# Rows of the first three expert passes fetched by token number, in a two-layer encoder with routed experts

## The reference

```python
def hier_moe(h, w_group, w_router, w_gate, w_up, w_down):
    """Top-1 expert group, then top-2 experts inside it; gated-MLP experts."""
    g_probs = softmax(t @ w_group); g_sel = argmax(g_probs)
    e_logits = (t @ w_router) of the chosen group     # 4 groups of 4 experts
    top_p, top_i = lax.top_k(softmax(e_logits), 2)
    weights = g_w * top_p / sum(top_p)
    a = jnp.einsum('td,edf->tef', t, w_gate)
    u = jnp.einsum('td,edf->tef', t, w_up)
    hid = jax.nn.silu(a) * u * gates[:, :, None]
    y = jnp.einsum('tef,efd->td', hid, w_down)
```

## Time and profile before

| | us |
|---|---|
| median of 3 runs | 1138.62 (1138.2 to 1141.27) |
| the profiled execution, its own time | 1140.07 |
| its span, first to last instruction | 1138.4 |
| mean granted TensorE clock | 0.972 of full speed |
| PE busy | 1050.2 |

### The profile page before, as it was taken

One profiled execution on the slowest core, in us unless ns is written; L12 is line 12 of the kernel. 1 busy time (PEld: TensorE's weight loads), 2 busy tenths in 40 slices (PEclk: granted clock), 3 DMA queues, 4 the chain that ended last, 5 costly groups with the idle time before them and its releaser, 6 DMA issues.

```text
span 1138.4 us, 16440 instructions
## 1 busy us (share of the span) xinstructions
PE 1050.2 (92%) x6553; PEld 662.3 (58%) x6553; DVE 446.1 (39%) x806; ACT 263.5 (23%) x528; POOL 240.5 (21%) x232
## 2 busy tenths in 40 slices
PE   4999999999999999978999998989998978999982
PEld 4989979989988877753333332454444443333321
DVE  6400314224226540155132226557547745232216
ACT  5132143134224411020011111314214510111111
POOL 5333314205214533003000005510000002000004
PEclk9999999999999999988999998989999998999997
DMA  7232223114115121367899887030004058998945
GB/s 305 74 130 75 75 90 114 56 42 161 56 37 168 37 74 74 148 278 285 313 358 376 353 361 259 42 148 0 1 1 148 1 233 339 333 380 323 403 189 222
DMA packets 34838, 201.01 MB, mean 177 GB/s; under 512 B 4352, under 2 KB 4352, under 8 KB 25808
## 3 DMA queue, kind: packets, MB, share of 16 engines
q1 hardware_dynamic: 21168, 151.26, 34.7%
q10 hardware_dynamic: 8864, 31.74, 7.9%
q0 software_dynamic: 4736, 17.04, 4.1%
HBM read 303.70 MB, written 28.44 MB: 292 GB/s over the span
## 4 chain that ended last, share of the span: by engine, by line
PE 79%; DVE 12%; issue 3%; DMA 2%; ACT 2%; POOL 1%; SPq 0%; POOLq 0%; DVEq 0%; ACTq 0%
PE ps L844 30%; PE ps L1083 15%; PE ps L1102 7%; PE ps L969 4%; PE ps L1207 4%; PE ps L1149 3%; PE ps L850 3%; DVE arena L2079 2%; PE ps L1071 2%; DVE arena L2076 2%; PE ps L1060 1%; PE ps L912 1%; ACT arena L1522 1%; PE ps L1167 1%; DMA ring<-in_w_ret 1%
## 5 line engine op out<-in xcount | busy, mean ns | idle before, releaser
L844 PE MATMUL ps<-x_hi,ring_r 128*128 128x264 f32 x1024 | 190.9, 287 | 3.2 <-DVE xT L1562 3.1
L2159 POOL TENSOR_TENSOR ring_r<-ring,ring_r 128x1024 fp32r<-128x1024 f32 x56 | 136.9, 2459 | 260.5 <-ACT ring_r L1299 260.4
L844 PEld LDWEIGHTS ps<-x_hi,ring_r 128*128 128x128 f32 x1024 | 160.3, 190 | 3.6 <-issue 3.3
L1083 PE MATMUL ps<-arena,xT 128*32 128x512 f32 x864 | 158.0, 600 | 0.0
L1083 PE MATMUL ps<-ring,xT 128*32 128x512 f32 x672 | 143.9, 602 | 5.9 <-DVE xT L1562 5.9
L844 PE MATMUL ps<-xT_r,ring_r 128*128 128x264 f32 x512 | 146.2, 286 | 0.0
L1562 DVE TENSOR_TENSOR xT<-ps,gains 128x512 f32<-128x512 f32 (+1 forms) x76 | 46.9, 660 | 182.8 <-PE ps L1071 177.3
L844 PE MATMUL ps<-ring_r,x_hi 128*128 128x512 f32 x320 | 100.6, 395 | 0.0
L844 PEld LDWEIGHTS ps<-xT_r,ring_r 128*128 128x128 f32 x512 | 97.0, 189 | 0.1
L1102 PE MATMUL ps<-arena 128*32 128x512 f32 x624 | 87.3, 595 | 4.3 <-ACT arena L1436 4.3
L1299 ACT ACTIVATE ring_r<-ring 128x1024 fp32r<-128x1024 f32 x56 | 57.9, 1054 | 118.4 <-PE ps L844 70.8
(11 more groups left out here) (265 smaller groups left out, 1554.7 us busy)
## 6 DMA issues: line engine op xcount, KB each, us to landing
arena<-in_w_gu SPq DMA_DIRECT2D x22, 2048.0 KB, 14.8
ring<-in_w_gu SPq DMA_DIRECT2D x20, 2048.0 KB
arena<-in_w_down SPq DMA_DIRECT2D x36, 1024.0 KB
arena<-in_w_gu POOLq DMA_DIRECT2D x18, 2048.0 KB
ring<-in_w_gu POOLq DMA_DIRECT2D x14, 2048.0 KB
arena<-in_w_down POOLq DMA_DIRECT2D x26, 1024.0 KB
ring<-in_w_ret SPq DMA_DIRECT2D x48, 512.0 KB, 3.7
ring<-in_w_ret_out SPq DMA_DIRECT2D x16, 512.0 KB, 4.9
```

Source lines behind the costliest of these rows:

```text
L844: last = mm(dst, a_parts[x], b_parts[y], start=(start and n == 0), stop=(stop and n == 2))
L1083: last = mm(ps[cols, b, :], xgT[:, k % 2, c, cols], by_row(gu(j))[:, c, :], start=(c == 0), stop=(c == KT - 1))
L2159: G.tensor_tensor(w_lo[slot][:, m], w_raw[slot][:, m], w_hi[to][:, m], ALU.subtract).then_inc(lo_made, 1)
```

## The change

- **Rows by token number.** ScalarE stores the normalized rows to device memory (token_rows), tile by tile, as soon as they are made. For each of passes 0, 1 and 2 VectorE makes a one-hot table of slots and tokens (slots_of_pass), PE multiplies it with a column of token numbers (tokens_of), ScalarE turns the result into integers, and POOL fetches the 128 rows with one indirect load (gather_rows). The product of the one-hot table with the rows, and ScalarE's copy of it, are gone. Passes 3 to 11 read slot_rows as before.
- **VectorE's order.** The places in the pairs are worked out first, from the pair counts alone, then pass 0's table, then the rows of e_of for the pairs, then the rest, with slot_i, pass 1's table, the rows of e_of for the singles, pass 2's table. Pass 0's rows are scaled by ScalarE.
- **POOL's order.** First gather, six scatters, second gather, the other scatters, the reading and loading for pass 0's singles, third gather.
- **Slots.** ROWS_SLOT becomes 5, so that pairs 3 and 4 of pass 2 are guessed and only pair 5 of pass 3 waits for the scatters. The first half of W_q (attention) is loaded behind the last gathers.
- **ScalarE.** The row load of pass 3 (load_rows(3)) stands ahead of the copy of pass 0's hidden values and waits for the scatters.
- **Products of constants.** Five ahead of the mask, five ahead of the token numbers, five behind them, instead of nine behind the ranks.

```diff
-ROWS_SLOT = 3
-GUESSED = [4, 5, 0, 1, 2]
+ROWS_SLOT = 5
+GUESSED = [0, 1, 2, 3, 4]
+GATHERED = 3
...
+                constant_products(5)
                 n = EXPERTS * (5 - l)
                 pe.wait_ge(m["mask_ready"], 1)
...
-                for _ in range(9):
-                    mm(ps[:, 4, :], ident, con[:, 0:512], start=True, stop=True)
-
-
-                pe.wait_ge(m["slot_ready"], 2)
-                for c in range(2):
+
+                def tokens_of(k):
+                    pe.wait_ge(hot_ready, GATHERED * l + k + 1)
                     for i, t in enumerate(tiles):
-                        last = mm(ps[:, c, :], one_hot[0:rows(t), t, :], xn[0:rows(t), t, 512 * c:512 * c + 512],
+                        last = mm(ps[:, B_TOKENS[k], 0:1], one_hot[k][0:rows(t), t, :], con[0:rows(t), C_TOKEN + t:C_TOKEN + t + 1],
                                   start=(i == 0), stop=(i == len(tiles) - 1))
-                last.then_inc(full[0], 1)
+                    last.then_inc(tokens_made, 1)
+
+                constant_products(5)
+                tokens_of(0)
+                constant_products(5)
...
+                        if k == 0 and c == KT // 2:
+                            tokens_of(1)
...
                 rows_to_features(0)
                 gate_up(0)
                 rows_to_features(1)
+                tokens_of(2)
...
+                def store_rows(n):
+                    t = MOE_TILES[l][n]
+                    act.wait_ge(nrm[f"_m{l}"]["xn_done"], n + 1)
+                    act.dma_start(token_rows[128 * t:128 * t + rows(t), :], xn[0:rows(t), t, :]).then_inc(rows_stored, 16)
...
-                fl.wait_full(act, f"X0_{l}")
-                nc.scalar.activation(xg[:, 0, :], flat(ps[:, 0:2, :]), ACT.Copy).then_inc(free[0], 1)
-                act.wait_ge(m["scattered"], 16 * 2 * (5 - l))
-                load_rows(1)
+                def tokens_of(k):
+                    act.wait_ge(tokens_made, GATHERED * l + k + 1)
+                    nc.scalar.activation(token_i[:, l, k:k + 1], ps[:, B_TOKENS[k], 0:1], ACT.Copy).then_inc(tokens_read, 1)
...
+                tokens_of(0)
+                first_features()
+                tokens_of(1)
                 tanh_of(0)
-                load_rows(2)
+                tokens_of(2)
                 for k in range(1, ROUNDS):
+                    if k == 1:
+                        act.wait_ge(m["scattered"], 16 * 2 * (5 - l))
                     load_rows(k + 2)
...
+                def gather_rows(k):
+                    pool.wait_ge(tokens_read, GATHERED * l + k + 1)
+                    if k == 0:
+                        pool.wait_ge(rows_stored, 16 * (5 * l + len(tiles)))
+                    if k == 2:
+                        round_full(pool, l, B_ROWS, 0)
+                    G.indirect_dma_start(xg[:, k % 2, :], None, token_rows,
+                                         bass.IndirectOffsetOnAxis(token_i[:, l, k:k + 1], 0)).then_inc(rows_gathered[k], 16)
```

More of the change, by code:

```diff
@@ L737, in first_weights @@
                     gate_up_weights(l, j, j)
-                rest = [j for j in (0, 1, 2, 4, 5) if j not in ready]
+                rest = [j for j in GUESSED if j not in ready]
                 for j in rest[:2]:
@@ new lines, in experts, with slots_of_pass @@
+                step.wait()
+                for n in range(2):
+                    step.done(V_.tensor_reduce(first_place[:, n, 0:nt], in_pairs[:, n], X, ALU.add))
+                step.wait()
+                iota = con[:, C_IOTA:C_IOTA + 128]
+                def slots_of_pass(k, where, numbers):
+                    for t in range(nt):
+                        step.done(V_.tensor_scalar(one_hot[k][:, t, :], numbers, where[:, 0, t:t + 1], None, ALU.is_equal))
+                    step.wait()
+                    for t in range(nt):
+                        last = V_.scalar_tensor_tensor(one_hot[k][:, t, :], numbers, where[:, 1, t:t + 1], one_hot[k][:, t, :],
+                                                       ALU.is_equal, ALU.add)
+                    last.then_inc(hot_ready, 1)
```

189 lines of the change are left out of this document (117 added, 72 removed).

## The result

The changed kernel takes 1143.8 us (median of 19 runs, 1140.66 to 1146.85), the kernel before 1138.53 (19 runs, 1137.04 to 1142.52): ratio 1.0039, 95% interval 1.003 to 1.0049. It is 0.4% **slower**; predicted was 1132.6. The profiled execution took 1144.62 (before 1140.07), its span is 1142.8 (before 1138.4).

A forecast was written before the change was run, and what follows sets the result against it. PE was taken as the bound, with a serial stretch ahead of the expert passes deciding pass 2's gate/up; 2.5 us earlier in layer 0 plus 3.5 in layer 1 made 6.0, so 1138.62 becomes 1132.6, range 1127.5 to 1138.5.

The forecast's parts named there:

- Products of constants, gain 1.1: Ahead of the mask: five constant products hold PE's clock up, so VectorE starts on the counts 1.1 us earlier.
- First table at 518.3: Layer 0's routing: VectorE has pass 0's one-hot table ready at 518.3 us, before it was 525.66.
- First gather, lands 5.2 after its issue: Pass 0's rows, layer 0: issued at 520.1, landing 525.3, bounds 3.1 to 7.3 us; pass 0's gate/up at 528.8.
- rival B: First gather waits for row stores behind guessed weights, starts at 524.5, pass 0 at 533; 1138 us, chance 0.15.
- slot_i at 528.1: Layer 0: the slot numbers are ready at 528.1 us, 4.9 later than before, as first-pass work goes ahead.
- Second gather at 536.0: POOL's queue, layer 0: seventh transfer, issued at 536.0, its numbers in time at 535.6, landing by 540.
- POOL's value loads are bare, 4.0 us: Ahead of pass 1: four value loads (3.2) and two issues (0.8) follow POOL's eleventh transfer; gate/up 1 at 546.0.
- rival C: POOL's loads cost next to nothing and the second gather's rows decide: pass 1 at 543, 1127 us, chance 0.05.
- Low clock at pass 1: 1.5 in layer 0, none in layer 1: Gate/up 1 starts at 1.2 GHz in layer 0, giving back 1.5 us; layer 1's shorter wait costs no clock.
- Third gather, hidden in both layers with 3.1 to 7.3 us: Pass 2's rows: in layer 0 issued at 546.2, landed by 553.5 beside slot-5 weights, needed at 554.9, so no wait.
- Rival D: Third gather beside slot-5 weights lands after 16.4 us; pass 2 comes 5 late, layer 1 5.8; 1149 us, chance 0.08.
- Passes 3 to 11 as before: Behind pass 2 nothing waits and all moves by the same amount; a wait there would make the forecast wrong altogether.

The follow-up runs named there:

- no_early_products: The changed kernel without the five products of constants ahead of the mask: 1145.39 us, ratio 1.0047 to the kernel before.
- hold_in_best: The fastest follow-up kernel (1132.08 us) with the slot-5 weights issued only when pass 3's rows have landed: 1135.18 us, ratio 0.9961 to the kernel before.
- rows3_late: The changed kernel with pass 3's row load issued behind ScalarE's copy of pass 0's hidden values: 1143.47 us, ratio 1.0041 to the kernel before.

## Why the prediction was wrong, point by point

- *Products of constants, gain 1.1.* Right in kind, 2.4 GHz at the rank products (1.21 instead of 2.21); size 2.0 in the trace of no_early_products, and its median can't confirm it.
- *First table at 518.3.* Right: 518.5.
- *First gather, lands 5.2 after its issue.* In layer 0 it took 6.5 (520.48 to 527.0), inside the bounds: 1.3 late. **In layer 1 it took 8.7**, outside them (the upper one was 7.3), for I had given layer 1 no landing of its own; pass 0's gate/up came 2.7 late there. It is not rival B, whose sign was POOL idle until the rows' stores land: POOL issued as soon as it had the numbers. ScalarE's copies took 2.18 (2.2 predicted). Pass 0's gate/up started 1.7 late and took 1.1 more than I had (it ended at 541.5): some five and a half of its sixteen half steps ran at 1.2 GHz, not three and a half as before; PE had stood 2.7 and 2.4 us ahead of it.
- *slot_i at 528.1.* Right to 0.1.
- *Second gather at 536.0.* 538.40: the numbers came 2.8 us late, from the two delays above, and four scatters stood behind them. I had named POOL's queue as the bound but not that a wait in its middle delays the scatters' end, and so the slot-5 weights.
- *POOL's value loads are bare, 4.0 us.* **Wrong.** The loads are issued between two scatters. The bound 0 was missing; I had taken SP's rows for another engine's. This is the mechanism of rival C, at 0.05, and so is its sign, gate/up 1 released by VectorE. By the Trainium skill (DMA: Bandwidth & Descriptors, "Latency and other measured facts") four of them would have cost 2.4 us; no run here shows what one takes, only that four add nothing here, where the issues behind them stand between the scatters. Pass 1 came at 545.7 against 546.0 because this error and the late second gather cancel in layer 0, which is luck. In layer 1 they don't, as the first gather took 3.5 longer than I had it: pass 1 gained 1.0 (1.3 with the 0.3 of layer 0), not 3.5.
- *Low clock at pass 1: 1.5 in layer 0, none in layer 1.* It came in both, 1.6 and 1.7. The gap of 2.5 us that I had read as leaving the clock up before holds 1.1 us of transposes; PE stood 1.47 in it.
- *Third gather, hidden in both layers with 3.1 to 7.3 us.* **The step that decided.** In layer 0 it was hidden, 4.5 us, for it was issued 2.6 us ahead of the weights; I had expected them beside it. In layer 1 it landed after 12.8. The range's ends came from scatters with quiet queues and from a load in another queue; the rows of loads beside weights went to 16.4, and I set them aside as "deep behind weights in the same kind of queue". Rival D had the place and the mechanism, at 0.08. Its price was 5.8 late against before in layer 1, and pass 2's gate/up came 5.9 late, but the agreement is luck: it had a landing of 16.4 and one of 11.3 as the point from which it decides, where the landing was 12.8, PE would have waited from 9.3 on, and the clock fell in the wait. Its like price for layer 0 did not come. The Trainium skill (DMA: Bandwidth & Descriptors, "SWDGE vs HWDGE vs iDMA") lets each DMA engine go round between the queues; the 8.3 us estimated from it was nearer than my bound but still too low.
- *Passes 3 to 11 as before.* **Wrong**, and named as what would make the forecast wrong altogether: 2.4 of layer 0's 2.7 us lost to pass 4's rows and to weights ahead of a down projection. I had read that nothing waits there before, and not how much slack there was.

In one line: predicted 2.5 and 3.5 earlier; layer 0 came 0.3 earlier and layer 1 4.7 later, the latter from 1.0 gained at pass 1, 7.1 lost at pass 2 and 1.4 back in the tail.

## What to carry to other kernels

A step that is moved earlier runs beside other transfers than before: take its landing from rows where those transfers run, and ask for each whether it is issued before or after the big stream that waits for the same event. A gain ahead of a pipeline of passes lasts only as far as the transfers have slack; look at the DMA share of the passes behind, not only at whether something waits there today. And where an engine's queue gets a wait in its middle, whoever needs the *last* instruction of that queue pays.

## What the runs showed of the hardware

- The third gather landed in 4.4 to 6.8 us in 21 of the 22 cases in which the 3 MB of weights were issued 1.9 us behind it or more (8.3 in one, layer 0 of hold_in_best), and in 11.3, 12.8 and 12.8 in layer 1 of rows3_late, the changed kernel and no_early_products, where they were issued 0.4 us behind it. A plain load of the same 512 KB, issued 0.3 us ahead of those weights, took 3.7, but plain loads of 256 KB with the same start took 3.5 to 9.7.
- The first gather, beside guessed weights already in flight, took 6.1 to 8.0 us in layer 0 and 6.9 to 9.7 in layer 1.
- POOL's direct loads are issued between indirect transfers that stand ahead of them in its program (541.98 and 542.38, while scatters start at 540.98, 542.25 and 543.51).
- Making products of constants faster can end them too soon: behind a gap of 4.47 us the next product ran at 0.55 of full speed for its first 3.5 us, behind one of 2.07 at full speed. Two more products behind the token numbers and two in a wait of 2.4 us kept 2.4 GHz and were together worth some 3 us.
